# Attention scores that stay in PSUM: bias added by TensorE, rows divided by their sums in the products that turn them

## What is computed

```python
s_loc = einsum('bqhd,bjwhd->bhqjw', q_r, k_r) * scale + bias
s_loc = where(col_valid, s_loc, NEG_BIG)
s_ctx = einsum('bqhd,bhld->bhql', q_r, k_ctx) * scale
p = softmax(concatenate([s_loc, s_ctx], -1), -1)
o = einsum(p_loc, v_r) + einsum(p_ctx, v_ctx)
```

## Time and profile before

| | us |
|---|---|
| median of 3 runs | 2026.12 (2019.57 to 2027.88) |
| profiled execution, its own time | 2030.75 |
| its span, first to last instruction | 2028.6 |
| TensorE busy, matmul / weight load | 1905.9 / 1718.9 |
| DVE, ACT, POOL busy | 1001.8, 939.8, 944.0 |
| mean granted clock of TensorE | 0.982 of full |

### The profile page before, as it was taken

One profiled execution on the slowest core, in us unless ns is written; L12 is line 12 of the kernel. 1 busy time (PEld: TensorE's weight loads), 2 busy tenths in 40 slices (PEclk: granted clock), 3 DMA queues, 4 the chain that ended last, 5 costly groups with the idle time before them and its releaser, 6 DMA issues.

```text
span 2028.6 us, 41739 instructions
## 1 busy us (share of the span) xinstructions
PE 1905.9 (94%) x17940; PEld 1718.9 (85%) x17940; DVE 1001.8 (49%) x1516; ACT 939.8 (46%) x1766; POOL 944.0 (47%) x767
## 2 busy tenths in 40 slices
PE   6899999999999989999988999999999998999997
PEld 2887878797899879999947878787879997899996
DVE  2574747475611255552057657475745133555502
ACT  4554645454533454443345555364554334544432
POOL 1434426170666626666416153342516664466663
PEclk9999999999999989999989999999999999999998
DMA  7314232232443314434453141413224432244442
GB/s 291 101 50 143 64 117 94 89 115 86 135 124 122 120 63 124 124 122 127 123 204 124 50 140 55 136 65 125 87 88 156 125 125 83 94 125 125 125 125 73
DMA packets 65414, 231.52 MB, mean 114 GB/s; under 512 B 7376, under 2 KB 11856, under 8 KB 64592
## 3 DMA queue, kind: packets, MB, share of 16 engines
q1 hardware_dynamic: 59040, 215.21, 33.3%
q10 hardware_dynamic: 6192, 13.66, 1.9%
HBM read 223.58 MB, written 5.26 MB: 113 GB/s over the span
## 4 chain that ended last, share of the span: by engine, by line
PE 79%; DVE 9%; ACT 4%; issue 3%; POOL 2%; DMA 2%; ACTq 1%; SPq 0%; DVEq 0%; POOLq 0%
PE psz L471 57%; PE psw L471 20%; DVE work L1360 3%; ACT work L954 3%; DMA ring<-in_w 2%; POOL ringlo L1735 1%; DVE work L1369 1%; PE psz L479 1%; PE psw L479 1%; ACT whi L954 1%; DVE rstd L1369 1%; DVE part L1360 1%; DVE work L1363 1%; POOL work L1771 1%; DVE work L1366 0%
## 5 line engine op out<-in xcount | busy, mean ns | idle before, releaser
L1735 POOL TENSOR_TENSOR ringlo<-ring,whi 128x512 fp32r<-128x512 f32 x608 | 811.1, 1357 | 756.7 <-ACT whi L954 756.7
L471 PE MATMUL psz<-hhi,whi 128*128 128x386 f32 x1696 | 587.1, 346 | 23.2 <-POOL ringlo L1735 14.5
L471 PE MATMUL psz<-hlo,whi 128*128 128x386 f32 x1696 | 577.6, 341 | 0.0
L471 PE MATMUL psz<-hhi,ringlo 128*128 128x386 f32 x1696 | 576.4, 340 | 0.0
L954 ACT ACTIVATE whi<-ring 128x1024 fp32r<-128x1024 f32 x304 | 320.2, 1053 | 133.4 <-PE psz L471 125.1
L471 PE MATMUL psw<-work 64*64 64x64 f32 (+4 forms) x9024 | 348.8, 232 | 17.6 <-issue 9.1
L471 PEld LDWEIGHTS psw<-work 64*64 64x64 f32 (+2 forms) x9024 | 294.5, 137 | 73.1 <-issue 55.6
L471 PEld LDWEIGHTS psz<-hhi,whi 128*128 128x128 f32 x1696 | 321.0, 189 | 36.1 <-issue 18.9
L471 PE MATMUL psz<-part,whi 128*128 128x386 f32 x1344 | 346.6, 339 | 3.2 <-DVE work L1360 1.5
L471 PEld LDWEIGHTS psz<-hlo,whi 128*128 128x128 f32 x1696 | 322.9, 190 | 2.1
L471 PEld LDWEIGHTS psz<-hhi,ringlo 128*128 128x128 f32 x1696 | 321.0, 189 | 0.0
(11 more groups left out here) (107 smaller groups left out, 1725.2 us busy)
## 6 DMA issues: line engine op xcount, KB each, us to landing
ring<-in_w SPq DMA_DIRECT2D x400, 512.0 KB, 3.5
pk<-in_pk ACTq DMA_DIRECT2D x8, 832.0 KB, 4.4
const<-in_const SPq DMA_DIRECT2D x1, 1795.0 KB, 10.0
work<-in_x SPq DMA_DIRECT2D x1, 1544.0 KB, 6.8
work<-in_x ACTq DMA_DIRECT2D x1, 1544.0 KB, 6.5
out_x<-work ACTq DMA_DIRECT2D x1, 1544.0 KB, 5.5
work<-out_x ACTq DMA_DIRECT2D x1, 1544.0 KB, 9.8
out_x<-work SPq DMA_DIRECT2D x4, 386.0 KB, 2.3
```

The costliest lines, as they stand in the source:

```text
L471: ins = nc.tensor.matmul(out, a, b, start=start, stop=stop, skip_group_check=True)
L1735: L.do(G.tensor_tensor(out, a, b, op), S[sig] if sig else None)
```

## The change

The scores no longer go to SBUF before the exponential. TensorE adds the bias itself: a third product into bank 4, with the identity as stationary and the bias columns as moving operand. DVE takes the maximum straight from PSUM, already negated, in one instruction. ACT's exponential reads bank 4 and writes SBUF. DVE then only takes the reciprocal of the row sums (`ri_ready`). ACT makes a diagonal matrix of them (`rdiag`, the identity scaled by row, `ridiag_ready`), and the transposes of `flip_mm` become full products of the rows with `rdiag`, which turn and divide at once. `scores_mm(j)` and `retain(0)` wait for `p_ready`, since bank 4 is read until the exponential is done; the wait for `bias_ready` moves from DVE to TensorE. The hunk left out only renames semaphores in a list.

```diff
--- before.py
+++ after.py
@@ -97,7 +97,7 @@
     "mi_done": 2, "mi_ready": 2, "nn_done": 2, "nn_ready": 4, "qh_done": 2, "qh_ready": 4,
     "ch_done": 3, "ch_ready": 3, "yv_done": 2, "y_done": 2, "y_copied": 4, "yc_ready": 1, "ysq_ready": 1, "gn_done": 2,
     "yroot_ready": 1, "o_ready": 1,
-    "sc_done": 6, "sctx_ready": 6, "s_ready": 6, "mx_ready": 6, "p_ready": 6, "pn_ready": 6, "pt_done": 6,
+    "sc_done": 6, "mx_ready": 6, "p_ready": 6, "ri_ready": 6, "ridiag_ready": 6, "pt_done": 6,
     "pt_ready": 6, "no_done": 6, "no_ready": 6,
     "dt_ready": 2, "de_ready": 2, "rope_done": 1, "rope_ready": 2, "kt_done": 1, "kt_ready": 4, "xi_ready": 2,
     "qx_ready": 2, "st_done": 4, "sd_ready": 4, "st0_ready": 4, "ry_done": 1, "ry_ready": 2, "rst_done": 1,
@@ -256,7 +256,7 @@
         qh = wk(12 * 64).rearrange("p (c t d e) -> p c t d e", c=2, t=3, d=2)
         dg = wk(12 * 64).rearrange("p (d g e) -> p d g e", d=2, g=6)
         st = wk(3 * 256).rearrange("p (n s d v) -> p n s d v", n=3, s=2, d=2)
-        fin = wk(2 * 64).rearrange("p (d v) -> p d v", d=2)
+        rdiag = wk(P)
         lwal, lgl = wk(TP), wk(TP)
         dtab = wk(2 * 384).rearrange("p (h c) -> p h c", h=2)
         s0 = wk(2 * 128).rearrange("p (d v) -> p d v", d=2)
...
@@ -609,20 +609,25 @@
                                 freed(zb + 4)
                                 pe.wait_ge(*at_of("sig_ready", p, 3))
                             else:
-                                pe.wait_ge(*at_of("s_ready", p, j - 1))
+                                pe.wait_ge(*at_of("p_ready", p, j - 1))
                             if kind == 0:
                                 mm(w(4, 0, P), q, nk[rows(hb), 0:P], sig="sc_done")
                             else:
                                 mm(w(4, 0, P), q, pk[rows(hb), PK["kc"]:PK["kc"] + P])
-                                mm(w(4, P, 256), q, nk[rows(hb), LAT:TP], sig="sc_done")
+                                mm(w(4, P, 256), q, nk[rows(hb), LAT:TP], True, False)
+                                if j == 1:
+                                    pe.wait_ge(*at_of("bias_ready", p, 0))
+                                a = PK["bias"] + 384 * hb + (P if kind == 1 else 0)
+                                mm(w(4, P, 256), ident, pk[:, a:a + 256], False, True, "sc_done")
 
                         def flip_mm(j):
                             n = 3 if JOBS[j][1] else 1
-                            pe.wait_ge(*at_of("pn_ready", p, j))
+                            pe.wait_ge(*at_of("ridiag_ready", p, j))
                             if j:
                                 pe.wait_ge(*at_of("no_ready", p, j - 1))
                             for i in range(n):
-                                tr(w(5, i * P, P), scores[j % 2][:, i * P:(i + 1) * P], "pt_done" if i == n - 1 else None)
+                                mm(w(5, i * P, P), scores[j % 2][:, i * P:(i + 1) * P], rdiag,
+                                   sig="pt_done" if i == n - 1 else None)
 
                         def values_mm(j):
                             hb, kind = JOBS[j]
@@ -650,7 +655,7 @@
 
                         def retain(i):
                             if i == 0:
-                                pe.wait_ge(*at_of("s_ready", p, 5))
+                                pe.wait_ge(*at_of("p_ready", p, 5))
                                 freed(zb + 7)
                                 freed(zb + 9)
                                 mm(w(4, 0, 256), perm, tq[:, LAT:TP])
@@ -1105,9 +1110,10 @@
                                 n = 3 if JOBS[i - 2][1] else 1
                                 act.wait_ge(*at_of("pt_done", p, i - 2))
                                 run(ptr[:, 0:n, :], w(5, 0, n * P).rearrange("p (k q) -> p k q", k=n), sig="pt_ready")
-                            if i < 6:
-                                act.wait_ge(*at_of("sc_done", p, i))
-                                run(scores[i % 2][:, 0:P], w(4, 0, P), sig="sctx_ready")
+                            if 1 <= i <= 6:
+                                j = i - 1
+                                act.wait_ge(*at_of("ri_ready", p, j))
+                                run(rdiag, ident, ACT.Copy, "ridiag_ready", scale=ri[:, j % 2:j % 2 + 1])
 
                         def values(j):
                             hb, kind = JOBS[j]
@@ -1117,8 +1123,8 @@
                         def powers(i):
                             if i < 6:
                                 act.wait_ge(*at_of("mx_ready", p, i))
-                                s_ = scores[i % 2][:, 0:384 if JOBS[i][1] else P]
-                                run(s_, s_, ACT.Exp, "p_ready", bias=mx[:, i % 2:i % 2 + 1], accum_out=rs[:, i % 2:i % 2 + 1])
+                                n = 384 if JOBS[i][1] else P
+                                run(scores[i % 2][:, 0:n], w(4, 0, n), ACT.Exp, "p_ready", bias=mx[:, i % 2:i % 2 + 1], accum_out=rs[:, i % 2:i % 2 + 1])
 
                         def retain(i):
                             if i == 0:
@@ -1559,26 +1565,12 @@
 
                             if 1 <= i <= 6:
                                 j = i - 1
-                                s_ = scores[j % 2]
-                                n = 384 if JOBS[j][1] else P
                                 dve.wait_ge(*at_of("p_ready", p, j))
-                                recip(ri[:, j % 2:j % 2 + 1], rs[:, j % 2:j % 2 + 1])
-                                L.settle()
-                                ts(s_[:, 0:n], s_[:, 0:n], ri[:, j % 2:j % 2 + 1], sig="pn_ready")
+                                recip(ri[:, j % 2:j % 2 + 1], rs[:, j % 2:j % 2 + 1], "ri_ready")
                             if i < 6:
-                                hb, kind = JOBS[i]
-                                s_ = scores[i % 2]
-                                dve.wait_ge(*at_of("sctx_ready", p, i))
-                                if kind:
-                                    a = PK["bias"] + 384 * hb + (P if kind == 1 else 0)
-                                    if i == 1:
-                                        dve.wait_ge(*at_of("bias_ready", p, 0))
-                                    tt(s_[:, P:384], w(4, P, 256), pk[:, a:a + 256], ALU.add)
-                                    L.settle()
-                                n = 384 if kind else P
-                                L.do(V.tensor_reduce(mt[:, 0:1], s_[:, 0:n], AX.X, ALU.max), S["s_ready"])
-                                L.settle()
-                                ts(mx[:, i % 2:i % 2 + 1], mt[:, 0:1], -1.0, sig="mx_ready")
+                                dve.wait_ge(*at_of("sc_done", p, i))
+                                L.do(V.tensor_reduce(mx[:, i % 2:i % 2 + 1], w(4, 0, 384 if JOBS[i][1] else P), AX.X, ALU.max,
+                                                     negate=True), S["mx_ready"])
 
                         def retain(i):
                             if i == 0:
```

More of the change, by code:

```diff
@@ L327, in trunk @@
             nn_ready no_done no_ready o_ready out_k out_st p_ready p_step pend_ready pk_in
-            pn_ready prm_in pt_done pt_ready qh_done qh_ready qx_ready rgn_done ro_ready
+            ri_ready ridiag_ready prm_in pt_done pt_ready qh_done qh_ready qx_ready rgn_done ro_ready
             rope_done rope_ready row_done row_ready rows_clear rr_ready rroot_ready rsq_ready
-            rst_done rst_ready rt_root ry_done ry_ready ryc_ready s_ready sc_done scan_ready
-            sctx_ready sd_ready sig_ready silu_c sq_ready sq_used sum_used ss_done st0_ready st_done
+            rst_done rst_ready rt_root ry_done ry_ready ryc_ready sc_done scan_ready
+            sd_ready sig_ready silu_c sq_ready sq_used sum_used ss_done st0_ready st_done
             til_ready tv_ready u_done u_ready v_step vt_done vt_ready w_hi w_lo w_used wm_done x_ld x_st wm_ready
```

## The result

The changed kernel takes 2075.4 us (median of four runs, 2072.1 to 2079.9) against 2024.4 us for the kernel before (four runs, 2019.6 to 2027.9). The ratio is 1.0255, 95% interval 1.0225 to 1.0285. It is slower, as forecast, but by 51 us where 31 were forecast, and outside the range given (2041 to 2069). The profiled execution took 2079.93 us, its span is 2078.0, 49.4 more than the span before. The question is where the 18 us beyond the sum went.

What follows compares the result with a forecast made beforehand. TensorE was taken to bound the kernel: added products and a level 1 stall sum to 3.87 us per pair, times 8 = 31 us, giving 2061.7 from the profiled execution, 2057 as a median; range 2041 to 2069.

Steps and rivals of the forecast that it cites:

- rival 2: DVE and ACT set the levels, so their savings leave the path: 21 us faster, 2005; chance 0.04.
- Rival 3: Turning by products costs what transposes cost and biases fall into waits: under 8 us, 2030; chance 0.06.
- (a): Bias by TensorE: four 256-column products per pair inside running groups, 0.47 us each, bounds 0.42 and 0.52.
- (b): Turning by products with rdiag, per pair: four flips of three at +0.35 us, two of one at +0.12.
- dense stretch: Attention work inside the dense products ahead of level 1: two biases and one single flip, +1.06 us per pair.
- Rival 1: Biases and flips cost only their streamed columns, with no new wait: 18 us, 2044; chance 0.12.
- Step (d): Level 1: TensorE waits some 0.7 us in scores_mm(4) for job 3's delayed exponential, bounds 0.3 and 1.2.
- Rival 4: Stops near state products shift and the clock halves in four more stages: 8 us on top, 2065; chance 0.10.
- my own main case: The forecast of 2057 us, including the level 1 stall in every pair stage; chance 0.68.
- the known terms: Biases, flips and level 1 stall at their bounds: 20 to 39 us in all, giving 2046 to 2065.

Runs made afterwards that it cites:

- e9_psum_only: Changed kernel, but DVE divides rows, transposes turn them, and the bias is left out; scores stay in PSUM: 2026.3 us, ratio 0.9996.
- e5_turn_only: Kernel before with only the turning and dividing by products with rdiag, ACT ordered as in e1_order: 2031.5 us, ratio 1.0036.
- e1_order: Changed kernel with rdiag of job 2 and job 3's exponential put behind the copy of job 1's values on ACT: 2055.1 us, ratio 1.015.
- e2_load: Changed kernel with a small extra exponential on ACT ahead of the wait for ri_ready(2), loading the table early: 2054.9 us, ratio 1.0159.
- e7_wait_alone: Kernel before with a tiny square root on ACT ahead of the copy of job 1's values, delaying it by a table load: 2042.6 us, ratio 1.0086.
- e3_transposes: e1_order with transposes in place of the products with rdiag, row division left out: 2039.3 us, ratio 1.0063.

## Why the prediction was right and wrong

**The bound: right.** TensorE sets the levels. DVE's saving of 48 us brought 0.08 us a stage: e9_psum_only has it without the adds, negations and copies, and e5_turn_only, without the normalisations, shows no gain either. So rival 2 fell. Rival 3 fell too: every bias and every flip was paid.

**Prices (a) and (b): right.** Bias, taken at 0.47 between 0.42 and 0.52: measured 0.45 to 0.47. Flip of three, +0.35: +0.37 to +0.39, just over its upper bound of 0.37. Single flip, +0.12: +0.13 to +0.15. By the rule of the Trainium skill that the prediction quoted ("TensorE: Matmul & The Clock Gate", section Terms) the flips of three would have cost +0.48, an estimate; the rows stand nearer to the trace's sum. The dense stretch was forecast at +1.06 and measured at +1.01, level 2 +0.59 and +0.64, levels 3 and 4 +0.35 each and +0.40 and +0.38. The products together make 3.17 a stage by the forecast, and 4.89 - 1.64 = 3.25 by measurement, 26 us of the whole. Rival 1, the stream price with no wait, fell with them.

**Step (d), the moved waits: the step that failed.** The order of ACT's work was right to a few tenths of a us, as the rows of the result show. Two things were wrong in what followed from it. First, I asked only who waits for the exponential, scores_mm(4). The exponential is also what the values' copy of job 1 queues behind, and flip_mm(2), which stands ahead of scores_mm(4) on TensorE, waits for that copy:

```
 pe.wait_ge(*at_of("ridiag_ready", p, j))
 if j:
     pe.wait_ge(*at_of("no_ready", p, j - 1))
```

The second wait is in the code before too, and was never last there. I had TensorE finishing the flip of three at 354.15 and waiting from then on; in truth it could not begin it. The stall is 1.64 us in place of 0.70, and beyond my upper bound of 1.2, since that bound stretched each ACT step but kept the wrong waiter. That is 0.94 x 8 = 7.5 us. e1_order and e2_load take it away in two ways, and e7_wait_alone makes it without the rest.

Second, I gave the new wait no consequence for the clock. Rival 4 had the right kind of event, half clock behind a stop of TensorE, and a size that came near by luck (four more stages, 8 us; it was five stages and 9.4 us), and the wrong place: it hung on the stops near the state products, which did not grow, and the chance of 0.10 was set for that. The fall came behind the wait that my own main case forecast, in the middle of the levels. The two terms are 7.5 + 9.4 = 17 us, and the forecast's 31 with them 48 of the 49.4 in the span.

**The range.** Its upper end, 2069, lay 4 us above the bounds of the known terms (2065) and had no room for rival 4's 8 us on top of them. With the stall of 1.64 the forecast's own sum would have been 2065 without the clock and 2074 with it. A wait whose size depends on a queue's order deserved an upper bound from the whole queue.

**What stays open:** why the fall follows the same wait in some stages and not in others, whether the bias products have a part in that, and what sets the length of the stretch behind the last turn.

## What to carry to other kernels

When an engine gets a new wait, walk everything that is queued behind it, and for every entry list all its waiters, not only the one whose semaphore was edited; a wait that is never last today becomes the last one when its signal moves. An ACT table load or a copy behind such a wait belongs to its length, and changing the order of three steps on ACT was worth 20 us here. Work that is moved onto the bounding engine pays its whole price even where another is relieved of 48 us.

## What the runs showed of the hardware that I had not expected

A wait of TensorE of 1.5 to 1.65 us between groups of FP32 products in level 1 was followed by half clock in 13 of 32 stages, at 1.5 to 3.1 us of lost time each; without that wait the levels of 80 stages all ran at full clock. Turning a 128x128 block by an FP32 product costs 0.13 us more than by a transpose in place (e1_order less e3_transposes, three for 0.37 to 0.39), where a stream of columns had put it at 0.05 to 0.10.
